# Prompt attention of a hybrid decoder step: the next tile's projections in six half pieces between the heads' products, and x turned one tile further ahead

## The reference, cut to what matters

```python
h = rmsnorm(x)                        # x: 1024 x 1024
q, k, v = h @ w_in[:, :1536]          # 16 heads x 64 | 4 x 64 | 4 x 64
# tiles of 128 tokens; each sees its own keys and those of the tile ahead
s = einsum(q, kk) * 64 ** -0.5 + bias # per kv head g: 4 query heads, 256 keys
p = softmax(concat([s, sink]))[..., :-1]
o_att = einsum(p, vv)                 # then rmsnorm'd by its own mean square
```

## Time and profile before

| what | us |
|---|---|
| median of three runs (4509.46, 4512.47, 4513.96) | 4512.47 |
| the profiled execution | 4509.16 |
| its span, first to last instruction | 4507.1 |
| TensorE busy in it | 3888.5 |
| VectorE, ScalarE, GpSimd busy | 2506.4, 1299.0, 1381.6 |

### The profile page before, as it was taken

How to read it: one execution, slowest core, us unless ns; L and a number is a source line. 1 busy time by engine, 2 the same in 40 slices (tenths; PEclk the granted TensorE clock), 3 DMA queues, 4 the chain that set the end, 5 groups by cost and what they waited for, 6 DMA issues and landing times.

```text
span 4507.1 us, 42180 instructions
## 1 busy us (share of the span) xinstructions
PE 3888.5 (86%) x11725; PEld 2009.5 (45%) x11725; DVE 2506.4 (56%) x5496; ACT 1299.0 (29%) x3863; POOL 1381.6 (31%) x1267
## 2 busy tenths in 40 slices
PE   8998589998698789999789999889999888887776
PEld 4556245543353345454345554344554344443332
DVE  2333255555411377754477764577765468766664
ACT  2333022322100122342232342233334233333332
POOL 0000033321000043434433444433444344334442
PEclk9887699998798899999999999999999999999999
DMA  5000100000723399999999999999999999999997
GB/s 195 19 19 10 55 14 10 19 14 20 290 81 122 121 415 418 418 414 420 421 403 414 410 420 414 421 419 401 412 419 417 421 419 395 419 419 401 419 420 291
DMA packets 223915, 1312.43 MB, mean 291 GB/s; under 512 B 24809, under 2 KB 41230, under 8 KB 90033
## 3 DMA queue, kind: packets, MB, share of 16 engines
q0 software_dynamic: 148608, 1082.20, 58.0%
q1 hardware_dynamic: 75112, 228.01, 13.3%
HBM read 1283.71 MB, written 28.49 MB: 291 GB/s over the span
## 4 chain that ended last, share of the span: by engine, by line
DMA 27%; PE 24%; DVE 7%; issue 3%; ACT 3%; DVEq 1%; ACTq 0%; POOL 0%; POOLq 0%
DMA ex_ring<-in_expert_uv,ex_idx 26%; PE psum L2743 15%; DVE ex_ring L3128 4%; PE psum L2772 3%; PE psum L2721 3%; ACT ex_diag L2924 1%; PE psum L2791 1%; ACT ex_weight L2919 0%; PE psum L2816 0%; PE psum L2833 0%; DMA ex_ring<-in_expert_uv,ex_idxT 0%; POOL ex_ring L2663 0%; DVE ex_top_at L3023 0%; DMA pair_p<-scratch_mixed 0%; ACT ex_dots L2915 0%
## 5 line engine op out<-in xcount | busy, mean ns | idle before, releaser
L2743 PE MATMUL psum<-ex_ring,ex_diag 128*128 128x512 f32 x4096 | 1917.7, 612 | 331.3 <-ACT ex_diag L2924 310.0
L3128 DVE CUSTOM_DVE_ANT_0 ex_ring<-ex_ring,ex_x_rows 128x1024 f32<-128x1024 f32 x1024 | 1250.7, 1226 | 832.5 <-DMA ex_ring<-in_expert_uv,ex_idx 767.9
L2663 POOL DMA_INDIRECT ex_ring<-in_expert_uv,ex_idx x1024 | 1157.3, 1130 | 1730.0 <-PE psum L2743 1530.7
L2743 PEld LDWEIGHTS psum<-ex_ring,ex_diag 128*128 128x128 f32 x4096 | 771.5, 194 | 1301.8 <-issue 848.5
L2915 ACT ACTIVATE ex_dots<-ex_dots 128x2 f32<-128x2 f32 x512 | 104.1, 203 | 1795.8 <-DVEq L3131 1795.4
L2924 ACT ACTIVATE ex_diag<-ident,ex_weight 128x128 f32<-128x128 f32 x1024 | 355.0, 393 | 36.9 <-issue 1.7
L1029 PE MATMUL psum<-w_zx,ssd_hT 128*128 128x512 f32 (+1 forms) x768 | 303.6, 551 | 3.4 <-issue 1.8
L2721 PE MATMUL psum<-ex_xT,ex_chunk 128*128 128x256 f32 (+1 forms) x1280 | 276.5, 360 | 4.2 <-ACT ex_sub L2900 2.9
L2721 PEld LDWEIGHTS psum<-ex_xT,ex_chunk 128*128 128x128 f32 x1280 | 229.0, 191 | 97.7 <-issue 77.1
L2919 ACT ACTIVATE ex_weight<-ex_gates,ex_dots 128x1 f32<-128x1 f32 x1024 | 246.1, 287 | 35.7 <-issue 0.3
L1029 PEld LDWEIGHTS psum<-w_zx,ssd_hT 128*128 128x128 f32 x768 | 139.9, 196 | 166.0 <-issue 164.8
(11 more groups left out here) (465 smaller groups left out, 3867.9 us busy)
## 6 DMA issues: line engine op xcount, KB each, us to landing
ex_chunk<-in_route_wq SPq DMA_DIRECT2D x80, 512.0 KB, 7.9
ex_chunk<-in_w_out SPq DMA_DIRECT2D x48, 512.0 KB, 8.5
ex_ring<-in_expert_uv,ex_idx POOLq DMA_INDIRECT x1024, 20.5
ex_chunk<-in_read_wq SPq DMA_DIRECT2D x24, 512.0 KB, 8.0
ex_chunk<-in_w_mo SPq DMA_DIRECT2D x24, 512.0 KB, 7.9
w_zx<-in_w_in SPq DMA_DIRECT2D x1, 10304.0 KB, 29.2
w_out<-in_w_out SPq DMA_DIRECT2D x2, 4096.0 KB
w_out<-in_cache_mem_k SPq DMA_DIRECT2D x8, 1024.0 KB, 12.7
```

The lines of the kernel that those rows point to most:

```text
L2663: nc.gpsimd.indirect_dma_start(out=ring[:, n % RING, :], out_offset=None, in_=io["expert_uv"], in_offset=bass.IndirectOffsetOnAxis(ap=idx[ ...
L2743: ins = nc.tensor.matmul(psum[c][:], diag[:, q % 3, s, :], ring[:, n % RING, D + c * BANK:D + (c + 1) * BANK], start=(n % SLOTS == 0), sto ...
L3128: nc.vector.tensor_tensor_reduce(ring[:, n % RING, 0:D], ring[:, n % RING, 0:D], x_rows[:, tile % 3, :], 1.0, 0.0, ALU.mult, ALU.add, dots ...
```

## The change

On TensorE `project` takes a part: four of the eight accumulating products in each half, the waits on weights and hT at the first half, the signals at the second. The turn is written out anew: a half product ahead of scores 0, between scores 0 and 1, behind scores 1, behind scores 2, behind scores 3 and behind turn_p 2. `turn_q` follows the last half, `mix 2` and `turn_p 3` as before.

`rows` now works for tile v = t + 2, and stands at the end of turn t, between turn_k and mix 3; `rows(1)` goes ahead of turn 0. VectorE's and ScalarE's parts of it (`rows`, `squares`) move to the end of their turns too, and GpSimd's factor of the mean square is one tile further ahead. The loops run over turns 1 to 5, and turn 6 is written out.

```diff
--- before.py
+++ after.py
@@ -292,17 +292,20 @@
                 pe.drain()
                 pe.sem_inc(x_seen.sem, 1)
 
-            def project(c, u, first_use=False):
-
-                if first_use:
+            def project(c, part, u, first_use=False):
+
+                if first_use and part == 0:
                     pe.wait_ge(w_in[c], 16)
-                if c == 0:
+                if c == 0 and part == 0:
                     pe.wait_ge(hT_ready.sem, hT_ready.this(u, 2))
-                out, full = begin(f"p{c}", u)
-                for b in range(DB):
+                f, bank, out = fill(f"p{c}")
+                if part == 0:
+                    begin(f"p{c}", u)
+                for b in range(4 * part, 4 * part + 4):
                     ins = nc.tensor.matmul(out[:], hT[:, b, :], w_qkv[:, b, c * BANK:(c + 1) * BANK], start=(b == 0), stop=(b == DB - 1))
-                ins.then_inc(full, 1)
-                if c == 2:
+                if part:
+                    ins.then_inc(f.full[bank], 1)
+                if c == 2 and part:
                     pe.drain()
                     pe.sem_inc(projected.sem, 1)
 
@@ -361,26 +364,37 @@
                 pe.drain()
                 pe.sem_inc(mixed.sem, 1)
 
-            def turn(t, u, first=False):
+            def turn(t, u, v, first=False):
                 front = u is not None
                 if front:
-                    rows(u)
+                    project(0, 0, u)
                 scores(t, 0, first)
+                if front:
+                    project(0, 1, u)
                 scores(t, 1, first)
-                for g in range(KV):
-
-                    if front and g < 3:
-                        project(g, u)
-                    if front and g == 3:
-                        turn_q(u)
-                    if g > 0:
-                        mix(t, g - 1, first)
-                    turn_p(t, g, first)
-                    if g + 2 < KV:
-                        scores(t, g + 2, first)
+                if front:
+                    project(1, 0, u)
+                turn_p(t, 0, first)
+                scores(t, 2, first)
+                if front:
+                    project(1, 1, u)
+                mix(t, 0, first)
+                turn_p(t, 1, first)
+                scores(t, 3, first)
+                if front:
+                    project(2, 0, u)
+                mix(t, 1, first)
+                turn_p(t, 2, first)
+                if front:
+                    project(2, 1, u)
+                    turn_q(u)
+                mix(t, 2, first)
+                turn_p(t, 3, first)
                 if front:
                     turn_k(u)
-                mix(t, KV - 1, first)
+                if v is not None:
+                    rows(v)
+                mix(t, 3, first)
 
             front_fills.prime(pe)
             back_fills.prime(pe)
@@ -397,13 +411,16 @@
             pe.wait_ge(far_row, 1)
             nc.tensor.matmul(psum[6][0:HEADS, 0:384], table, onehot, start=True, stop=True).then_inc(multiplied, 1)
             for c in range(3):
-                project(c, 0, first_use=True)
+                for part in range(2):
+                    project(c, part, 0, first_use=True)
             turn_q(0)
             turn_k(0)
-            turn(0, 1, first=True)
-            with pe.Fori(1, TILES - 1) as t:
-                turn(t, t + 1)
-            turn(TILES - 1, None)
+            rows(1)
+            turn(0, 1, 2, first=True)
+            with pe.Fori(1, TILES - 2) as t:
+                turn(t, t + 1, t + 2)
+            turn(TILES - 2, TILES - 1, None)
+            turn(TILES - 1, None, None)
 
         @block.scalar
         def _(act):
@@ -466,10 +483,8 @@
                 act.drain()
                 act.sem_inc(pT_ready.sem, 1)
 
-            def turn(t, u, first=False):
+            def turn(t, u, v, first=False):
                 front = u is not None
-                if front:
-                    squares(u)
                 for g in range(KV):
                     exponentials(t, g, first)
                     if front and g < 2:
@@ -477,6 +492,8 @@
                     turned_p(t, g, first)
                     if front and g == 2:
                         turned_q(u)
+                if v is not None:
+                    squares(v)
 
                 act.wait_ge(o_ready.sem, o_ready.this(t))
                 nc.scalar.activation(junk[:], o[:], ACT.Square, accum_out=oms[:])
@@ -489,10 +506,12 @@
             for c in range(2):
                 queries(c, 0)
             turned_q(0)
-            turn(0, 1, first=True)
-            with act.Fori(1, TILES - 1) as t:
-                turn(t, t + 1)
-            turn(TILES - 1, None)
+            squares(1)
+            turn(0, 1, 2, first=True)
+            with act.Fori(1, TILES - 2) as t:
+                turn(t, t + 1, t + 2)
+            turn(TILES - 2, TILES - 1, None)
+            turn(TILES - 1, None, None)
 
         @block.gpsimd
         def _(pool):
@@ -513,12 +532,15 @@
             pool.sem_inc(rstd_ready.sem, 1)
             pool.sem_inc(orstd_ready.sem, 1)
             factor(ms, rstd, ms_ready, rstd_ready, 0)
-            with pool.Fori(0, TILES - 1) as t:
-
-                pool.wait_ge(kv_ready.sem, kv_ready.this(t))
-                factor(ms, rstd, ms_ready, rstd_ready, t + 1)
+            pool.wait_ge(kv_ready.sem, kv_ready.this(0))
+            factor(ms, rstd, ms_ready, rstd_ready, 1)
+            with pool.Fori(0, TILES - 2) as t:
+
+                pool.wait_ge(kv_ready.sem, kv_ready.this(t + 1))
+                factor(ms, rstd, ms_ready, rstd_ready, t + 2)
                 factor(oms, orstd, oms_ready, orstd_ready, t)
-            factor(oms, orstd, oms_ready, orstd_ready, TILES - 1)
+            for t in range(TILES - 2, TILES):
+                factor(oms, orstd, oms_ready, orstd_ready, t)
 
         @block.vector
         def _(dve):
@@ -649,10 +671,12 @@
             keys_values(0)
             next_keys(0, first=True)
             next_values(0, first=True)
-            turn(0, 1, first=True)
-            with dve.Fori(1, TILES - 1) as t:
-                turn(t, t + 1)
-            turn(TILES - 1, None)
+            rows(1)
+            turn(0, 1, 2, first=True)
+            with dve.Fori(1, TILES - 2) as t:
+                turn(t, t + 1, t + 2)
+            turn(TILES - 2, TILES - 1, None)
+            turn(TILES - 1, None, None)
             scaled(TILES - 1)
```

## The result

| | us |
|---|---|
| before, median of four runs | 4510.97 (4509.09 to 4513.96) |
| changed kernel, median of four runs | 4481.61 (4480.57 to 4486.51) |
| ratio, with its 95% interval | 0.9936 (0.9924 to 0.9948) |
| span of the profiled execution | 4480.6, against 4507.1 |

The change saves 29 us, 0.64%. It lies in the range, at nearly twice the 16.4 us of the forecast, between the forecast's case and rival B.

A forecast was written before the change was run, and what follows sets the result against it. TensorE's own order of work, slowed by its clock, was taken to bound the prompt attention stage. 5 x 2.2 + 7.15 = 18.2, less 1.8, gives 16.4 us saved: 4496 us, range 4472 to 4507.

The forecast's parts named there:

- the forecast's case: Prompt attention: the clock falls at four to six of six turn ends; 4496 us, own range 4490 to 4503, chance 0.62.
- rival B: Turn ends in prompt attention: the shorter stretch keeps the clock up throughout; gain 41 us, 4471 us; chance 0.17.
- Softmax slack, DMA, factor: Heads 0 to 2 keep 4 us slack or more; x's load, squares and factor fit in time: no new wait.
- Rival D: Softmax chain becomes the bound, heads 0 to 2 stalling like head 3, 4.3 us a turn; 4525 us; chance 0.08.
- The stall: Before head 3's transposes of p, waiting for the exponentials: 1.43 us a turn stays, zero gained, zero lost.
- Where the gain comes from: Turn ends: about 10 us without dense products instead of 23.4, scores at full clock; 2.2 us a turn despite a fall.
- the one on x: Turn's end: x's transposes follow kv's; 0.2 us bank wait taken, VectorE's hT copies hidden beside head 3's p·v and the loop.
- The price of a fall: At a turn's end, half clock lasting into the first half product costs 4.9 us against 7.15; five falls in six.
- The last tile: End of the prompt attention stage, 406 to 450 us: at half clock throughout, stays so.
- Splitting: Three more switches a turn between dense and other products, 0.1 us each; with the bank's 0.2, 1.8 us over six turns.
- Rival C: Clock comes back late, first half product and head 0's scores at half clock, 8.9 against 7.15; 4505 to 4515; chance 0.13.
- The page of the Trainium skill: Transposes don't count as busy for full clock, so the clock falls at all six turn ends; gain 11 us.

## Why the prediction was right, and where not

*What bounds the stage.* Right: TensorE at a clock below full. The forecast has 47.64 us for a turn at full clock, and 47.62 was measured. That the two agree to 0.02 is luck: the measured turn ends at the short gap of the written-out turn, and inside the loop it is 47.9 (47.90 with whole projections, scores at 95.63 and 143.53). So half clock cost nearer 6.9 us a turn than 7.15.

*Softmax slack, DMA, factor.* Right: no wait of heads 0 to 2 in turns 0 to 6, and none for x. Rival D had no part in it.

*The stall.* 1.43 forecast as staying, 1.38 measured. But I priced it as 1.4 us of waiting; filled with useless work it gave back 12 us. Its cost was the clock that fell behind it.

*Where the gain comes from.* Right for a part, and wrong for the whole. The forecast credited the shorter stretch, and within it the scores moved behind the first half product: 2.2 us a turn, 6 x 2.2 - 1.8 = 11.4 with six falls. The kernel with x behind mix 3 has just that and six falls, and is 13 us faster than the kernel before. The step that failed is the one on x. Its transposes between kv's and mix 3 were taken for hidden, and the sum has no term for their place. Measured, that place alone (with the copies, squares and factor that go with it), in the old order with the scores where they were, brings 27 to 31 us in the medians of its two sets of runs (4485.86 and 4480.86; four of the twelve runs at 4503). In the changed order it is the 18 us from 4499.69 to 4481.61. Since x ahead alone is as fast as both together, the two parts don't add up.

*The price of a fall.* This is the mis-sized term. Five falls in six turn ends were forecast and five came, in turns 0 to 4. I took 4.9 us for each, with half clock lasting into the first half product. Of the five, three were over after 3.4 us (turns 0, 1 and 3, two of these with a second one of 3.4 us), one lasted 10.2, one 13.6. In all 41 us at half clock for 6 x 17 = 102, so 61 x 0.42 = 26 us saved where the forecast has 18.2. Turn 0 gives 1.3 of it back by its wait of 1.29 us for hT at 44.09, which the forecast missed because it looked only at turns of the loop. Head 3's transposes of p in turn 6 begin 24.4 us earlier (404.70 and 380.32).

*The last tile* was taken as unchanged. It began its half clock late, 12 us less of it, and from those transposes to the last product takes 43.7 us instead of 47.3: 3.6 saved. 26 - 1.3 + 3.6 = 28.3, for the 28.0 us seen.

*Splitting* was priced at 1.8 us and cost nothing that the traces show: 47.62 us a turn at full clock with whole projections and with halves.

*Rival C* (the clock comes back late, and the first scores are at half) did not come. Nearest was turn 4, where the clock came back 6.2 us into the half product of 6.75, beyond the 3.0 to 4.6 of the forecast; the scores behind it took 1.99. *Rival B* happened in turns 5 and 6, and turn 0, with 3.4 us at half clock, came near it. The 4471 of rival B lies just outside the stated range, which was meant to leave out only its lowest tail.

*The page of the Trainium skill* ("TensorE: Matmul & The Clock Gate", "Part 4: PE-mode transpose": transposes don't count as busy for the full clock) would have made it 11 us. The runs don't bear it out: 12 transposes in the stall kept the clock at full from 50 to 370 us, as narrow matrix products did (4469.87 and 4469.43, for 4481.61 with the stall empty), and doubling x's transposes cost nothing on balance. In these runs float32 transposes did count.

*Open*: how x's transposes ahead of mix 3 hold the clock or bring it back. In the changed order their place is worth 15 us of clock, while transposes and narrow products do equally well in the stall; and in four runs of twelve the old order had them there to little use. A little less idle time (the wait for hT comes right behind) may be one reason; no run tried it alone.

## What to carry to other kernels

Where the traces show an engine's clock falling behind a gap, price that gap by what runs slower after it, not by its length, and look for real work that can stand in it (here turn_q, one line up) before cutting or moving large pieces. A kernel whose clock takes one of two courses needs several runs: one median can hide a good course and a bad one 30 us apart. And try each half of a two-part change alone: here the part that looked like housekeeping, priced at nothing, did as much by itself as both together.

## What the runs showed of the hardware that was not expected

- With the same instructions and the same waits, TensorE's clock took either of two courses: 69 and 148 us of half clock in one stage in the two profiles, and 4472 to 4486 or 4503 us in all over twelve runs.
- A fall may be over after 3.4 us, before any 512-column product has come, with transposes alone in it, the last of p's, kv's and x's (turn 1: p·v at 130.60 again at full clock).
- Extra work on TensorE, 84 transposes or 42 narrow products in seven stalls, made the program 12 us faster; another 48 in the last tile 13 us.
